# Three parts of a dense expert product in two steps, where it was four parts in three

## What is computed

```
idx, gate = top-16 of (v1 + v2) per head, softmax          # 128 experts for each token
act = einsum(expert_down[idx], h)                          # one dot product for each expert
w   = gate * gelu(act)
x  += einsum(w, expert_up[idx])                            # weighted sum of 128 rows of 2048
```

## Time and profile before

| | us |
|---|---|
| median of 3 runs | 3905.32 (3898.13 to 3908.63) |
| the profiled execution's own time | 3898.68 |
| its span | 3896.9 |
| TensorE busy | 3272.8 (84% of the span) |
| VectorE busy | 2610.8 (67%) |
| GpSimd busy | 1256.0 (32%) |

### The profile page before, as it was taken

The page is one execution under the profiler, slowest core; times in us unless marked ns, Lnnn a source line. Parts: engine busy times, 40 slices in busy tenths (PEclk is TensorE's granted clock), DMA queues, the critical chain, the costliest instruction groups (busy, mean ns, idle before and its releaser), DMA issues.

```text
span 3896.9 us, 42007 instructions
## 1 busy us (share of the span) xinstructions
PE 3272.8 (84%) x14020; PEld 1678.1 (43%) x14020; DVE 2610.8 (67%) x5342; ACT 724.5 (19%) x1674; POOL 1256.0 (32%) x1133
## 2 busy tenths in 40 slices
PE   8998998999998886557888899989988874568888
PEld 7343344444875553112222268457855541122222
DVE  3877785565578889987555332524788899975563
ACT  1222223310111114451000002221111134520000
POOL 0000000000234545565445400001254455675553
PEclk9999999999999998667999999979999986689999
DMA  6343332234679999899999963424899998999998
GB/s 221 112 120 108 116 123 99 93 127 168 257 298 397 395 396 378 301 380 373 370 399 391 355 221 99 151 66 175 303 401 385 388 355 299 354 380 393 381 387 322
DMA packets 316854, 1075.59 MB, mean 276 GB/s; under 512 B 94332, under 2 KB 103436, under 8 KB 214668
## 3 DMA queue, kind: packets, MB, share of 16 engines
q0 software_dynamic: 147456, 728.77, 48.2%
q1 hardware_dynamic: 134240, 335.05, 24.2%
q10 hardware_dynamic: 34960, 9.27, 1.1%
HBM read 1415.93 MB, written 2.10 MB: 364 GB/s over the span
## 4 chain that ended last, share of the span: by engine, by line
PE 46%; DMA 23%; DVE 19%; issue 7%; POOL 2%; SPq 1%; ACT 1%; ACTq 0%; DVEq 0%; POOLq 0%; another core or an unknown queue 0%
DMA big<-in_peer_down,sc 9%; PE bank L750 9%; PE bank L1174 6%; DMA big<-in_peer_u,sc 6%; DMA wring<-in_dense_up 5%; DVE sc L2371 5%; PE bank L764 4%; PE bank L1113 4%; PE bank L1235 4%; DVE sc L2374 3%; PE bank L991 3%; PE bank L1157 3%; PE bank L915 2%; PE bank L980 2%; POOL big L684 2%
## 5 line engine op out<-in xcount | busy, mean ns | idle before, releaser
L2371 DVE CUSTOM_DVE_ANT_0 sc<-big,hs 128x1024 f32<-128x1024 f32 x480 | 587.8, 1225 | 429.7 <-DMA big<-in_peer_down,sc 226.7
L1235 PE MATMUL bank<-big,sc 128*32 128x512 f32 x4096 | 630.4, 702 | 181.9 <-DMA big<-in_peer_up,sc 85.0
L2374 DVE CUSTOM_DVE_ANT_0 sc<-big,hs,sc 128x1024 f32<-128x1024 f32 x480 | 616.7, 1285 | 17.1
L1174 PE MATMUL bank<-wring 128*128 128x512 f32 x1024 | 528.2, 651 | 113.0 <-DMA wring<-in_dense_up 92.5
L1157 PE MATMUL bank<-ht,wring 128*128 128x256 f32 x2048 | 505.7, 399 | 1.4 <-ACT wring L1620 0.9
L1157 PEld LDWEIGHTS bank<-ht,wring 128*128 128x128 f32 x2048 | 389.6, 197 | 191.7 <-issue 134.7
L750 PE MATMUL bank<-wring,ht 128*128 128x512 f32 x1024 | 468.9, 613 | 0.0
L684 POOL DMA_INDIRECT big<-in_peer_down,sc x256 | 311.9, 1218 | 372.3 <-DVE sc L2374 224.8
L684 POOL DMA_INDIRECT big<-in_peer_u,sc x256 | 319.5, 1248 | 337.2 <-DVE sc L2374 186.7
L1174 PEld LDWEIGHTS bank<-wring 128*128 128x128 f32 x1024 | 188.3, 199 | 451.5 <-issue 321.1
L684 POOL DMA_INDIRECT big<-in_peer_up,sc x256 | 302.1, 1180 | 244.9 <-PE bank L1235 144.0
(11 more groups left out here) (436 smaller groups left out, 3619.4 us busy)
## 6 DMA issues: line engine op xcount, KB each, us to landing
wring<-in_w_in SPq DMA_DIRECT2D x84, 1024.0 KB, 5.7
wring<-in_dense_down SPq DMA_DIRECT2D x64, 1024.0 KB, 9.0
wring<-in_dense_up SPq DMA_DIRECT2D x256, 256.0 KB
wring<-in_w_out SPq DMA_DIRECT2D x32, 1024.0 KB, 5.1
wring<-in_w_attn_o SPq DMA_DIRECT2D x16, 1024.0 KB, 5.0
wring<-in_peer_w_query SPq DMA_DIRECT2D x16, 1024.0 KB, 9.0
wring<-in_peer_w_q SPq DMA_DIRECT2D x16, 1024.0 KB, 5.5
wring<-in_glu_w_a SPq DMA_DIRECT2D x8, 1024.0 KB, 5.0
```

The source lines that it names most:

```text
L1174: mm = pe.matmul(dense_out[t][:, :], dense_w[:, r, t * P:(t + 1) * P], sup[:, m % 2, r % 4, :], start=(r == 0), stop=(r == DENSE - 1))
L1235: mm = pe.matmul(acc_bank[j][32 * q:32 * q + 32, :], w_blocks[:, u % 2, g, :], gslot[:, m % RING, q * 512:(q + 1) * 512], start=(u % PH == ...
L2371: st.link(v.tensor_tensor_reduce(dot_out[:, 0:cut_at], row[:, 0:cut_at], h[:, u // PH, 0:cut_at], 1.0, start, ALU.mult, ALU.add, acc))
L2374: v.tensor_tensor_reduce(dot_out[:, cut_at:D], row[:, cut_at:D], h[:, u // PH, cut_at:D], 1.0, start, ALU.mult, ALU.add, acc).then_inc(dot ...
```

## The change

One line, the schedule of the dense `up` parts:

```diff
 def up_part_at(n):
-    return min(max(n - FIRST_UP, 0) * 4 // 3, 4 * DENSE)
+    return min(max(n - FIRST_UP, 0) * 3 // 2, 4 * DENSE)
```

## The result

The changed kernel takes 3957.65 us (median of 4 runs, 3949.02 to 3965.92) against 3906.98 us of the kernel before in the same comparison: a ratio of 1.0127, with a 95% interval of 1.0108 to 1.0146. It is 50 us slower, where 15 us faster was forecast. The profiled execution is the longest of the four (3965.92 us, span 3964.2), so lengths read from it are some 8 us long in sum.

The account below looks back on a forecast made before the run. Bytes were taken to bound the stretches before step 257, TensorE the tails. Later starts (10.4 and 9.5 us) against shorter tails gave -7.1 and -7.8 us, -15 in all: 3890.4 us; forecast's own range 3883 to 3893, whole range 3879 to 3912.

Parts of the forecast that it names:

- That stretch is bound by bytes.: Layer 0, first part to step 257: DMA engines 0.99 busy at 384 GB/s, so moving TensorE work there gains nothing itself.
- The cost is from 0 to 37 us a layer ... I take 2 us: Two slabs span 5.33 steps, not 6; bytes need 25.2 us, a turn took 27.5; slabs were expected to land sooner.
- The rival of the turn: Before step 257, slabs land no sooner: turn 26.7 us, 22 us more a layer, 3935 us; chance 0.17 for turns above 26.1.
- Later slabs, 6.4 and 5.5 us: Slab bytes left at step 257 must come before it: 2.45 MB in layer 0, 2.1 MB in layer 1, delaying step 257.
- Range 0, 2 us a layer: End of range 0: TensorE's wait for VectorE's addition grows from 4.7 to about 7.3 us, taken as 2 us a layer.
- Tail of layer 0, 36.5 us: Step 257 to next block's product: 54.0 us becomes 36.5, with the next block's weights taking 27% of the bytes.
- the case of half of the bytes: Tail of layer 0: the next block's weights take half of the bytes, so the gathers need 42.6 us.
- Tail of layer 1, 25.8 us: 18 row sums and 8.28 MB of gathers left; 9.3 MB at 384 GB/s plus 1.5 us give 25.8 in place of 43.1.
- the forecast's sign: In the tails, TensorE waits for `up` gathers and the DMA share is above 0.95.
- The sum of a layer: Later start of step 257 plus the shorter tail: net -7.1 us in layer 0 and -7.8 us in layer 1.

Follow-up runs that it names:

- four-buffer kernel: The changed kernel with four slab buffers in place of two: 3893.92 us, 0.9964 of the kernel before.
- with the addition first: The changed kernel with four slab buffers, and VectorE's addition placed ahead of its dot product of that step: 3879.01 us, 0.9929 of the kernel before.

## Why the prediction was wrong, step by step

- **"That stretch is bound by bytes."** This reading of the earlier trace rows is where it went wrong. The share of 0.99 was true, but the turn of 27.5 us in the earlier trace rows was just as long as the bytes of its six steps needed, (2.1 + 6 x 1.42) MB at 384 GB/s, 27.7 us. Two bounds stood side by side, and I took the one and let the other give way. After the change the bytes alone would have allowed 25.2 us.
- **"The cost is from 0 to 37 us a layer ... I take 2 us"** for the turn. This is the term that failed. It measured 439.3 - 404.7 = 35 us in layer 0, nearly the upper bound, and 425.6 - (379.0 + 9.5) = 37 us in layer 1, on top of the 2 us that each of these sums already holds. The reason given, that the gather queue would run dry and leave its place to the slab, did not come true: the landings in the chain of layer 0 took 10.1 to 12.6 us, and before the change 10.3 to 12.7. In the turns looked at, the DMA share drops while TensorE works through a slab, and is full again when the next slab is on its way (0.68, then 1.02).
- **The rival of the turn** was the right one, at a chance of 0.17. Its time, 3935 us, was also too short (3957.65 measured), as it shortened the turn to 26.7 us; 27.5 would have given 440 us for a stage and some 55 us more than before in all. Its signs came true: a share of 0.92 where 0.96 or less was named, and 78.4 us of slab waits where more than 46 was.
- **Later slabs, 6.4 and 5.5 us.** Not seen alone, but the stage of the four-buffer kernel, 403.4 us against 404.7, bears out the sum of which they are the largest term.
- **Range 0, 2 us a layer.** The lengthened wait was forecast at 7.3 us and, with the slab wait out of the way, measured 6.28. Its price is not known by itself. Taking out nearly all the waits for additions of all ranges gave 0.35% (some 14 us) at the new schedule and 0.10% (4 us) at the old; the difference, about 10 us, is what the 4 us of the forecast answer to, and it is within the noise. In the changed kernel itself the wait was 0.4 us, and its removal gained nothing.
- **Tail of layer 0, 36.5 us.** It measured 34.6. SyncE's queue took 4.52 of 13.62 MB, 33%, where 27% was counted, and the gathers left were 9.08 MB, where 9.8 was. The two errors cancel, which is luck. The 27% came from mean packet sizes of the profile, and those mix rows with the small records; within the dense stage, while both queues had work, it was 24%. The weights are 6.82 MB by the trace and not 6.55; with that the case of half of the bytes is 43.3 us and not 42.6.

```profile
q0 software_dynamic: 1778, 9.08, 66.9%
q1 hardware_dynamic: 2382, 4.52, 34.8%
```

- **Tail of layer 1, 25.8 us.** It measured 31.8. The bytes were right (8.56 MB of gathers against 8.28), the rate was not: the share was 0.84, where the forecast's sign was above 0.95. GpSimd issued the last gather at 3943.24 us, and the engines then ran empty while the last row sums were made.

```profile
3941.90:3946.90 5.00, 5.00 (x28) 0.74 (x20) 2.74 (x4) 0.00 (x0) 0.99 (x1) 0.57 1.02 421
3946.90:3951.90 5.00, 2.13 (x20) 0.32 (x16) 2.49 (x4) 0.00 (x0) 0.00 (x0) 1.00 0.91 374
3951.90:3956.90 5.00, 3.60 (x20) 0.36 (x16) 0.26 (x1) 0.00 (x0) 0.00 (x0) 0.66 0.39 129
```

- **The sum of a layer.** From the first part to the next block's product it was 394.3 + 10.4 + 36.5 = 441.2 us; the changed kernel needed 473.3, the four-buffer one 441.1, and with the addition first 434.9. In layer 1 it was 379.0 + 9.5 + 25.8 = 414.3 us, against 456.9, 419.5 and 414.6. The arithmetic held to about 1% for a kernel that does not wait for its slabs.

## What to carry to other kernels

Before moving work forward into a stretch where the DMA engines are full, look for closed loops through it (buffer free, issue, landing, use), multiply the loop by the number of its turns, and compare that with the stretch. If the two are nearly equal, do not count on the loop to give; here it gave nothing, and the work moved in lengthened the stretch. A share near 1 says that the bytes are a bound, not that they are the only one. The cure was room or earlier release, not another schedule: four buffers, or the same space released by halves, turned 1.27% slower into 0.3 to 0.4% faster, and with the addition ahead of the dot product into 0.7%.

## What the runs showed of the hardware

While two queues of the DMA engines both had work, they moved similar numbers of packets (616 and 730 in 12.6 us, 137 and 155 in 4.4, but also 141 and 312 in 6.3), roughly as if by turns of equal numbers of rows. 1 MB in rows of 2 KB took 13 to 16 us from its first issue against gathers with rows of 8 KB, whether issued as four DMAs over 4 us, over 1.8 us, or as one. In rows of 8 KB the same MB moved in 4.4 and 6.3 us, and TensorE's matmuls no longer waited for it in layer 0; the kernel was 0.8% faster, some 32 us. So the length of the rows decided how a load fared against another queue, even where the engines were full either way.

A wait also costs what follows it: after 5.83 us without work TensorE's granted clock was 0.50, and the first part took 3.78 us in place of 1.91.
